# Four output buffers and eight-entry tables of destinations in the expert stage of a two-layer decoder, on one NeuronCore

## The chip, the cores and the metric

The kernel runs on one NeuronCore of a Trainium2 chip. TensorE (PE) multiplies matrices, VectorE (DVE) and ScalarE (ACT) compute and copy, GpSimd (POOL) here issues the indirect DMAs, and SyncE (SP) issues the plain ones. Each engine runs its own stream of instructions and waits for semaphores of the others. The metric is the device time of one execution in microseconds (us), as the median of the runs.

## The reference

Two decoder layers on 2048 tokens and 16 meta tokens with 1024 features. Each layer is an attention (windowed in the first, latent in the second) followed by a mixture of experts. The change is in the experts:

```python
g_p, g_idx = lax.top_k(g_prob, 1)                    # 1 of 4 groups
e_p, e_idx = lax.top_k(e_prob, TOP_K)                # 2 of its 8 experts
weights = g_p * e_p / jnp.sum(e_p, axis=-1, keepdims=True)
...
def expert_block(args):                              # w_gate, w_up: 1024x256, w_down: 256x1024
    xb, e = args
    return (jax.nn.silu(xb @ w_gate[e]) * (xb @ w_up[e])) @ w_down[e]
y = jax.ops.segment_sum(y_buf[dest] * sw[:, None], st, num_segments=T)
```

Each token goes to 2 of 32 experts; their outputs, times the token's share, are added to its row of the residual `h`.

## The kernel before

A layer's program is `project_and_route`, `experts`, `experts_beyond` (for experts with more than 160 tokens). `experts` takes the experts one after the other, 32 in layer 0 and 33 in layer 1 (`N`; the last one is a further block of an overfull expert), 160 token slots each (`CAP`; the first 128 and the other 32 are handled apart, as `x` and `xr`, `y` and `yr`). Every engine has its own `step(e)`, written as a pipeline: in step e

- PE flips the tokens of expert e (L1444, L1449), does gate and up of expert e-1 (L1461, `G` and `U`), and the down product of expert e-2 (L1475 to L1477 for 128 tokens, L1482 for the other 32). The down weights are used in two parts, `wd_hi` and `wd_lo`, which together hold them in full precision.
- ACT copies the flipped tokens (L1300, L1302), makes `wd_hi` of expert e-2 (L1309), the silu of e-1 (L1314), and half of the scaled output of e-2 (`y` L1320, `yr` L1322).
- DVE reads the list of e+2 (`find_sources`, L1339), copies flipped tokens (L1403), makes `wd_lo` of e-2 (L1329), writes the destinations and shares of e+1 (`find_places`, L1347 to L1349, semaphore `listed`), makes `h` of e-1 (L1417 to L1422), and the other half of `y` of e-2 (L1427).
- POOL gathers the tokens of e+2 (L1265, L1267) and scatters expert e-2 (L1285, L1288): an indirect DMA that adds rows of `y` and `yr` to `h` in HBM at the places of `prow`. Before it issues one scatter it waits until the scatter ahead has landed (L1283), since two that add to the same row must not overlap.
- SP loads the slots of e+2 (L1222, L1224), the gate and up weights of e (L1248, L1249) and the down weights of e-1 (L1254), 1 MB each, into rings of four buffers. It waits for `listed` of expert e-2 ahead of the slots, and for the gate and up product of e-4 ahead of the weights.

`At` holds the arithmetic of buffers: expert e has buffer e mod 2 (`slot`) or e mod 4 (`slot4`), and `uses`, `uses4` count how often that buffer was used before. `over_steps` writes the first steps out, runs the middle ones as a loop of `unroll` steps per turn, and writes out the last ones.

`prow` and `share` have four entries. The scatter of expert e-3 reads `prow` while it is issued, so DVE waits ahead of the destinations of e+1 until the scatter of e-3 has landed (L1346). `y` and `yr` have two buffers, so ACT and DVE wait ahead of expert g's output for the scatter of g-2 (L1317, L1425). `wd_hi` and `wd_lo` have one buffer: ACT waits ahead of the cast for the down product of g-1 (L1308).

Of the kernel before, what the change touches and what calls it, by code (L numbers as in the profile page):

```python
# [7 lines left out]
F32 = mybir.dt.float32  # L8
F32R = mybir.dt.float32r
# [41 lines left out]
class At:  # L51
# [1084 lines left out]
def experts(nc, io, dram, keep, layer):  # L1136


    with ExitStack() as ctx:
# [67 lines left out]
        with nc.Block() as block:  # L1207
# [49 lines left out]
            @block.gpsimd  # L1257
            def _(pool):
                def gather(e):

                    pool.wait_ge(sources, e.count(1, 1))
                    if e.after(4):
                        pool.wait_ge(flipped, e.back(4).count(3, 3))
                    pool.sem_inc(held, 1)
                    pool.indirect_dma_start(x[:, e.slot4, :], None, dram["xn"],  # L1265
                                            bass.IndirectOffsetOnAxis(ap=grow[:, e.slot4, 0:1], axis=0)).then_inc(x_in[e.slot4], 16)
                    pool.indirect_dma_start(xr[:, e.slot4, :], None, xn_parts,  # L1267
                                            bass.IndirectOffsetOnAxis(ap=grow[:, e.slot4, 1:2], axis=0)).then_inc(xr_in[e.slot4], 16)

                def step(e):  # L1270
                    if e.c == 0:
                        gather(e)
                        gather(e.back(-1))
                    if e.back(-2).live(N):
                        gather(e.back(-2))
                    f = e.back(2)
                    if f.live(N):
                        pool.wait_ge(y_act, f.count(2, 2))
                        pool.wait_ge(y_dve, f.count(1, 1))
                        pool.wait_ge(listed, f.count(1, 1))  # L1280
# [4 lines left out]
                        pool.indirect_dma_start(dram["h"], bass.IndirectOffsetOnAxis(ap=prow[:, f.slot4, 0:1], axis=0),  # L1285
                                                y[:, f.slot, :], None, bounds_check=ROWS - 1, oob_is_err=False,
                                                compute_op=ALU.add).then_inc(y_out[f.slot], 16)
                        pool.indirect_dma_start(h_parts, bass.IndirectOffsetOnAxis(ap=prow[:, f.slot4, 1:2], axis=0),  # L1288
                                                yr[:, f.slot, :], None, bounds_check=QN * ROWS - 1, oob_is_err=False,
                                                compute_op=ALU.add).then_inc(y_out[f.slot], 16)  # L1290
                over_steps(pool, 0, 2 + N, 6, EXPERTS - 2, step, unroll=4)
                for b in range(2):
                    pool.wait_ge(y_out[b], 32 * ((N + 1 - b) // 2))

            @block.scalar
            def _(act):
                def step(e):
                    if e.live(N):
                        act.wait_ge(flipped, e.count(3, 1))
                        nc.scalar.copy(xT[:, e.slot, 0:4, 0:P], T[:, e.c % 2, :].rearrange("p (c t) -> p c t", t=P)).then_inc(x_act, 1)  # L1300
                        act.wait_ge(flipped, e.count(3, 3))
                        nc.scalar.copy(xT[:, e.slot, :, P:CAP].rearrange("p (j k) t -> p k j t", k=DC // QN),  # L1302
                                       T[:, e.c % 2, 0:P * DC // QN].rearrange("p (k j t) -> p k j t", j=QN, t=REST)).then_inc(x_act, 1)
                    f, g = e.back(1), e.back(2)
                    if g.live(N):
                        act.wait_ge(d_in[g.slot4], (g.uses4 + 1) * 16)
                        if g.after(1):
                            act.wait_ge(downed, g.back(1).count(3, 3))  # L1308
                        nc.scalar.copy(wd_hi[:, :, :].rearrange("p c f -> p (c f)"), wd[:, g.slot4, :, :].rearrange("p c f -> p (c f)")).then_inc(d_high, 1)  # L1309
                    if f.live(N):  # L1310
                        act.wait_ge(gated, f.count(1, 1))
                        if f.after(2):
                            act.wait_ge(h_ready, f.back(2).count(1, 1))
                        nc.scalar.activation(act_g[:, f.slot, :, :].rearrange("p c t -> p (c t)"), G[:, f.slot, 0:FC * CAP], ACT.Silu).then_inc(silued, 1)  # L1314
                    if g.live(N):
                        if g.after(2):
                            act.wait_ge(y_out[g.slot], g.uses * 32)  # L1317
                        act.wait_ge(downed, g.count(3, 1))
                        act.wait_ge(listed, g.count(1, 1))
                        nc.scalar.activation(y[:, g.slot, 0:512], Y[:, g.c % 2, :], ACT.Copy, scale=share[:, g.slot4, 0:1]).then_inc(y_act, 1)  # L1320
                        act.wait_ge(downed, g.count(3, 3))
                        nc.scalar.activation(yr[:, g.slot, :], Y[:, g.c % 2, 0:QD4], ACT.Copy, scale=share[:, g.slot4, 1:2]).then_inc(y_act, 1)  # L1322
                over_steps(act, 0, 2 + N, 4, EXPERTS, step, unroll=4)

            @block.vector
            def _(dve):
# [15 lines left out]

                def find_places(e):

                    if e.after(4):
                        dve.wait_ge(y_out[e.slot], (e.uses - 1) * 32)  # L1346
                    nc.vector.tensor_scalar(prow[:, e.slot4, 1:2], slot[:, e.slot4, 1, 0:1], float(QN), quarter[:, :], ALU.mult, ALU.add)  # L1347
                    nc.vector.tensor_copy(prow[:, e.slot4, 0:1], slot[:, e.slot4, 0, 0:1])
                    nc.vector.tensor_copy(share[:, e.slot4, :], slot[:, e.slot4, :, 1].bitcast(F32))  # L1349
                    dve.drain().then_inc(listed, 1)  # L1350

                def along(t, of, width):
# [41 lines left out]
                def step(e):  # L1394
# [9 lines left out]
                    f, g = e.back(1), e.back(2)  # L1404
                    if g.live(N):
                        dve.wait_ge(d_high, g.count(1, 1))
                        low_part(wd_lo[:, :, :].rearrange("p c f -> p (c f)"), wd[:, g.slot4, :, :].rearrange("p c f -> p (c f)"),
                                 wd_hi[:, :, :].rearrange("p c f -> p (c f)")).then_inc(d_split, 1)
                    if e.back(-1).live(N):
                        find_places(e.back(-1))  # L1410
                    if e.turn is None and 1 <= e.c <= 10:
# [9 lines left out]
                        dve.drain()  # L1421
                        low_part(h_lo[:, f.slot, :, :], h[:, f.slot, :, 0:P], h_hi[:, f.slot, :, :]).then_inc(h_ready, 1)  # L1422
                    if g.live(N):
                        if g.after(2):
                            dve.wait_ge(y_out[g.slot], g.uses * 32)  # L1425
                        dve.wait_ge(downed, g.count(3, 2))
                        nc.vector.tensor_scalar(y[:, g.slot, 512:D], Y[:, (1 + g.c) % 2, :], share[:, g.slot4, 0:1], None, ALU.mult).then_inc(y_dve, 1)  # L1427
                over_steps(dve, 0, 2 + N, 12, EXPERTS - 4, step, unroll=4)

            @block.tensor  # L1430
            def _(pe):
                pe.wait_ge(consts, 32)

                def step(e):
# [30 lines left out]
                    if g.live(N):  # L1465
                        pe.wait_ge(d_split, g.count(1, 1))
                        pe.wait_ge(h_ready, g.count(1, 1))
                        for b in range(2):
                            if g.after(1):
                                pe.wait_ge(y_act if b else y_dve, g.count(2 if b else 1, 0))  # L1470
                            for k in range(FC):
                                hi, lo = h_hi[:, g.slot, k, :], h_lo[:, g.slot, k, :]
                                w = slice(512 * b, 512 * b + 512)
                                to = Y[:, (b + g.c) % 2, :]
                                nc.tensor.matmul(to, hi, wd_hi[:, k, w], start=(k == 0), stop=False)  # L1475
                                nc.tensor.matmul(to, hi, wd_lo[:, k, w], start=False, stop=False)
                                last = nc.tensor.matmul(to, lo, wd_hi[:, k, w], start=False, stop=(k == FC - 1))  # L1477
# [1103 lines left out]
```

## Time and profile before

| | |
|---|---|
| median of 3 runs | 3476.66 us (3474.6 to 3479.86) |
| the profiled execution's own time | 3475.05 us |
| its span, first to last instruction | 3473.2 us |
| granted TensorE clock, mean | 0.955 of full speed |
| PE, DVE, ACT, POOL busy | 3150.6, 1678.1, 1257.9, 1802.9 us |
| expert stage of layer 0, from the first slot load to the first instruction of the next stage | 885.9 to 1395.0 us |
| expert stage of layer 1, silus of the steps in the pipeline | 2940.2 to 3397.6 us |

A busy PE is a PE with matmuls in its pipeline, not one at its peak. Names begin with the stage: `ex_` is the expert stage, `aa_`, `pr_`, `pb_`, `ab_` and `fi_` are the others. Start times are counted from the span's start.

### The profile page before, as it was taken

To read this page: it belongs to the slowest core of one execution; us is meant where nothing else is said; L and a number is where in the kernel's file an instruction comes from. 1 tells how busy PE (TensorE), PEld (TensorE's weight loads), DVE (VectorE), ACT (ScalarE), POOL (GpSimd) and SP (SyncE) were. 2 spreads that over 40 slices of the span, in tenths; PEclk is the share of its full clock that TensorE was granted. 3 is DMA by queue.
4 is the path that set the end of the run, shared out by engine and by line. 5 is a ranking of instruction groups with operands and counts; after the bars stand their busy time and mean duration, and the time that the engine had idled before them with its cause. 6 is when DMAs were issued, how large, how long until landed. Compare 5 with 4: busy or idle time off the path is not lost. (4 is left out here: it accounts for less than half of the span.)

```text
span 3473.2 us, 56972 instructions
## 1 busy us (share of the span) xinstructions
PE 3150.6 (91%) x19621; PEld 2483.2 (71%) x19621; DVE 1678.1 (48%) x4096; ACT 1257.9 (36%) x2675; POOL 1802.9 (52%) x1447
## 2 busy tenths in 40 slices
PE   6999998899699998699799999999997996999992
PEld 4788886687588887699565666666665885888881
DVE  3555555577343333455365555555543663333333
ACT  2444444322122332344344444444433221322322
POOL 2655554244343333244488898888873223343344
PEclk8999999999899999799799999999999997999996
DMA  2001100843789995555602210222004545999985
GB/s 103 27 27 40 40 34 32 242 156 128 254 267 279 306 285 160 148 158 155 164 10 53 53 37 26 53 53 53 10 10 154 190 139 199 285 272 294 302 252 212
DMA packets 359637, 491.66 MB, mean 142 GB/s; under 512 B 87309, under 2 KB 286753, under 8 KB 357144
## 3 DMA queue, kind: packets, MB, share of 16 engines
q1 hardware_dynamic: 326136, 412.83, 38.0%
q0 software_dynamic: 33312, 76.43, 8.4%
q8 instruction: 104, 1.70, 0.2%
q14 instruction: 85, 0.70, 0.1%
HBM read 362.79 MB, written 135.09 MB: 143 GB/s over the span
## 5 line engine op out<-in xcount | busy, mean ns | idle before, releaser
L2117 POOL TENSOR_TENSOR ab_acc<-ab_acc,ab_pT 128x1024 f32<-128x1024 f32 (+2 forms) x320 | 593.9, 1856 | 91.7 <-ACT ab_pT L2151 53.6
L2151 ACT ACTIVATE ab_pT<-ab_S 128x512 f32<-128x512 f32 (+4 forms) x704 | 350.1, 504 | 515.2 <-PE ab_S L2242 249.8
L1285 POOL DMA_INDIRECT scratch_h<-ex_y,ex_prow x65 | 136.9, 2106 | 523.4 <-DVE ex_y L1427 370.9
L2174 DVE TENSOR_REDUCE ab_mx<-ab_W 128x2 f32<-128x800 f32 (+1 forms) x224 | 249.8, 1117 | 217.2 <-PE ab_W L2256 212.5
L1461 PE MATMUL ex_U<-ex_xT,ex_wu 128*128 128x160 f32 x2080 | 293.2, 299 | 0.0
L1461 PEld LDWEIGHTS ex_U<-ex_xT,ex_wu 128*128 128x128 f32 x2080 | 286.1, 190 | 0.0
L2240 PE MATMUL ab_S<-ab_q_hi,ab_k_hi 97*128 97x512 f32 (+4 forms) x704 | 276.0, 392 | 4.4 <-ACT ab_pT L2151 2.8
L2289 PE MATMUL ab_O<-ab_pT,ab_v 128*64 128x512 f32 (+3 forms) x1280 | 261.5, 547 | 0.0
L2241 PE MATMUL ab_S<-ab_q_lo,ab_k_hi 96*128 96x512 f32 (+4 forms) x704 | 255.1, 362 | 0.0
L2242 PE MATMUL ab_S<-ab_q_hi,ab_k_lo 96*128 96x512 f32 (+4 forms) x704 | 253.4, 360 | 0.0
L1085 PE MATMUL pr_PR<-pr_wo_hi,pr_o_hi 128*128 128x512 f32 x528 | 217.1, 411 | 38.0 <-DVE pr_wo_lo L950 33.5
L1347 DVE TENSOR_SCALAR ex_prow<-ex_slot,ex_quarter 128x1 int32<-128x1 int32 x65 | 13.8, 213 | 487.1 <-DMA scratch_h<-ex_yr,ex_prow 486.9
L333 POOL TENSOR_TENSOR aa_prob<-aa_prob,aa_rden 128x1024 f32<-128x1024 f32 x68 | 127.3, 1894 | 191.6 <-DVE aa_rden L500 191.6
L2256 PE MATMUL ab_W<-ab_k_hi,ab_q_hi 96*128 96x512 f32 (+5 forms) x704 | 206.5, 378 | 17.1 <-ACT ab_k_hi L2139 14.2
L1086 PE MATMUL pr_PR<-pr_wo_lo,pr_o_hi 128*128 128x512 f32 x528 | 211.1, 400 | 0.0
L1087 PE MATMUL pr_PR<-pr_wo_hi,pr_o_lo 128*128 128x512 f32 x528 | 211.0, 400 | 0.0
L2240 PEld LDWEIGHTS ab_S<-ab_q_hi,ab_k_hi 97*128 97x128 f32 x704 | 135.6, 193 | 87.3 <-issue 56.3
L2289 PEld LDWEIGHTS ab_O<-ab_pT,ab_v 128*64 128x64 f32 x1280 | 86.7, 139 | 139.9 <-issue 110.5
L1314 ACT ACTIVATE ex_act_g<-ex_G 128x320 f32<-128x320 f32 x65 | 28.4, 438 | 431.1 <-PE ex_U L1461 431.1
L589 PE MATMUL aa_PRJ<-aa_w_hi,aa_x_hi 128*128 128x512 f32 (+1 forms) x408 | 155.5, 381 | 16.3 <-DVE aa_w_lo L514 7.2
L2170 DVE CUSTOM_DVE_ANT_0 ab_junk<-ab_W,ab_mask 128x128 bf16<-128x128 f32 (+6 forms) x256 | 109.6, 466 | 125.1 <-PE ab_W L2256 123.8
L1329 DVE TENSOR_TENSOR ex_wd_lo<-ex_wd,ex_wd_hi 128x2048 fp32r<-128x2048 f32 x65 | 149.3, 2297 | 22.5 <-ACT ex_wd_hi L1309 22.3
(298 smaller groups left out, 7511.0 us busy)
## 6 DMA issues: line engine op xcount, KB each, us to landing
ex_wu<-in_moe_w_up SPq DMA_DIRECT2D x65, 1024.0 KB, 14.0
ex_wd<-in_moe_w_down SPq DMA_DIRECT2D x65, 1024.0 KB, 15.5
keep_wg<-in_moe_w_gate SPq DMA_DIRECT2D x33, 1024.0 KB, 8.0
ring_wg<-in_moe_w_gate SPq DMA_DIRECT2D x32, 1024.0 KB, 7.2
pr_o<-scratch_oT SPq DMA_DIRECT2D x33, 512.0 KB, 4.8
scratch_h<-pr_h SPq DMA_DIRECT2D x33, 512.0 KB, 5.1
scratch_xn<-pr_xn SPq DMA_DIRECT2D x33, 512.0 KB, 2.7
scratch_qT<-pb_qT SPq DMA_DIRECT2D x17, 768.0 KB, 5.2
```

What stands on the lines that cost most here:

```text
L1085: nc.tensor.matmul(PR[:, b, :], o_hi[:, i.slot, c, :], wo_hi[:, c, w], start=(c == 0), stop=False)
L1086: nc.tensor.matmul(PR[:, b, :], o_hi[:, i.slot, c, :], wo_lo[:, c, w], start=False, stop=False)
L1087: return nc.tensor.matmul(PR[:, b, :], o_lo[:, i.slot, c, :], wo_hi[:, c, w], start=False, stop=(c == DC - 1))
L1461: last = nc.tensor.matmul(out[:, f.slot, CAP * k:CAP * k + CAP], w[:, f.slot4, c, P * k:P * k + P], xT[:, f.slot, c, :], start=(c == 0), s ...
L2117: nc.gpsimd.tensor_tensor(to, to, pT[:, U % RING, :, 0:n], ALU.add).then_inc(added, 1)
L2151: nc.scalar.activation(pT[:, U % RING, h, 0:n], S[:, h, 0:n], ACT.Exp, scale=B_SCALE).then_inc(exped, 1)
L2174: nc.vector.reduce_max(mx[:, :, t, c:c + 1].rearrange("p h a -> p (h a)"), W[:, j % 2, :, 0:n], AX.X).then_inc(emptied, 1)
L2240: nc.tensor.matmul(to, k_hi[:, p % 2, h, kb], q_hi[:, p % 2, h, qs], start=True, stop=False)
L2241: nc.tensor.matmul(to, k_hi[0:QD, p % 2, h, kb], q_lo[:, p % 2, h, qs], start=False, stop=False)
L2242: last = nc.tensor.matmul(to, k_lo[:, p % 2, h, kb], q_hi[0:QD, p % 2, h, qs], start=False, stop=not diagonal)
L2256: last = nc.tensor.matmul(W[:, j % 2, h, 0:n], q_hi[0:QD, p % 2, h, P * t:P * t + P], k_hi[0:QD, p % 2, h, lo:lo + n], start=True, stop=True)
L2289: last = nc.tensor.matmul(O[HD * h:HD * h + HD, G % 2, 512 - n:512], values(U, h), pT[:, U % RING, h, 0:n], start=(U == opens[p, g]), stop ...
```

## The change

The tables `prow` and `share` get eight entries in place of four, `y` and `yr` four buffers in place of two (with four semaphores `y_out` for two), `wd_hi` and `wd_lo` two in place of one. Each wait that guards a buffer looks back as far as the new number of buffers says. The loops of POOL, ACT and DVE take eight steps per turn, so that the number of an entry is fixed in each written step; `uses4` is made right for that. PE's loop and SP's stay at four.

```diff
     @property
     def uses4(self):
 
-        return self.c // 4 if self.turn is None else self.turn + self.c // 4
+        return self.c // 4 if self.turn is None else self.turn * (self.unroll // 4) + self.c // 4
+
+    @property
+    def slot8(self):
+        return self.c % 8
...
-        wd_hi, wd_lo = s.sb("wd_hi", [P, FC, D], F32R), s.sb("wd_lo", [P, FC, D], F32R)
+        wd_hi, wd_lo = s.sb("wd_hi", [P, 2, FC, D], F32R), s.sb("wd_lo", [P, 2, FC, D], F32R)
...
-        prow = s.sb("prow", [P, 4, 2], I32)
-        share = s.sb("share", [P, 4, 2])
+        prow = s.sb("prow", [P, 8, 2], I32)
+        share = s.sb("share", [P, 8, 2])
...
-        y = s.sb("y", [P, 2, D])
-        yr = s.sb("yr", [P, 2, QD4])
+        y = s.sb("y", [P, 4, D])
+        yr = s.sb("yr", [P, 4, QD4])
...
-        y_out = s.sems("y_out", 2)
+        y_out = s.sems("y_out", 4)
...
                         d = f.back(1)
                         if f.after(1):
-                            pool.wait_ge(y_out[d.slot], (d.uses + 1) * 32)
+                            pool.wait_ge(y_out[d.slot4], (d.uses4 + 1) * 32)
...
-                over_steps(pool, 0, 2 + N, 6, EXPERTS - 2, step, unroll=4)
-                for b in range(2):
-                    pool.wait_ge(y_out[b], 32 * ((N + 1 - b) // 2))
+                over_steps(pool, 0, 2 + N, 6, EXPERTS - 2, step, unroll=8)
+                for b in range(4):
+                    pool.wait_ge(y_out[b], 32 * ((N + 3 - b) // 4))
...
-                        if g.after(1):
-                            act.wait_ge(downed, g.back(1).count(3, 3))
+                        if g.after(2):
+                            act.wait_ge(downed, g.back(2).count(3, 3))
...
-                        if g.after(2):
-                            act.wait_ge(y_out[g.slot], g.uses * 32)
+                        if g.after(4):
+                            act.wait_ge(y_out[g.slot4], g.uses4 * 32)
...
-                over_steps(act, 0, 2 + N, 4, EXPERTS, step, unroll=4)
+                over_steps(act, 0, 2 + N, 8, EXPERTS, step, unroll=8)
...
-                    if e.after(4):
-                        dve.wait_ge(y_out[e.slot], (e.uses - 1) * 32)
+                    if e.after(8):
+                        dve.wait_ge(y_out[e.slot4], (e.uses4 - 1) * 32)
...
-                        if g.after(2):
-                            dve.wait_ge(y_out[g.slot], g.uses * 32)
+                        if g.after(4):
+                            dve.wait_ge(y_out[g.slot4], g.uses4 * 32)
...
-                over_steps(dve, 0, 2 + N, 12, EXPERTS - 4, step, unroll=4)
+                over_steps(dve, 0, 2 + N, 12, EXPERTS - 4, step, unroll=8)
```

The rest of the diff puts the new buffer numbers into the operands.

No instruction changes its place among its engine's others; what changes is which semaphore some of them wait for, and after how many steps a loop turns. First VectorE in layer 0, from its `wd_lo` of expert 6 to its half of that expert's output, in step 8. A semaphore's number was used by an earlier stage, and the rows give it that stage's name: `aa_copied_dve` and `aa_copied_act` are `y_out[0]` and `y_out[1]`, `aa_summed` and `aa_o_ready` are the two new ones. Before:

```order
L1329 TENSOR_TENSOR ex_wd_lo<-ex_wd,ex_wd_hi 128x2048 [waits aa_sink_exped]
L1347 TENSOR_SCALAR ex_prow<-ex_slot,ex_quarter 128x1 [waits aa_copied_dve]
L1348 COPY ex_prow<-ex_slot 128x1
L1349 COPY ex_share<-ex_slot 128x2
L1381 TENSOR_REDUCE ex_ahead<-ex_grid 1x32
L1382 TENSOR_SCALAR ex_whose<-ex_whose 1x32
L1417 TENSOR_TENSOR ex_h<-ex_act_g,ex_U 128x320 [waits aa_exped,aa_scaled]
L1420 CAST ex_h_hi<-ex_h 128x256
L1329 TENSOR_TENSOR ex_h_lo<-ex_h,ex_h_hi 128x256
L1427 TENSOR_SCALAR ex_y<-ex_Y,ex_share 128x512 [waits aa_scaled,aa_copied_act]
```

The same place of the changed kernel:

```order
L1333 TENSOR_TENSOR ex_wd_lo<-ex_wd,ex_wd_hi 128x2048 [waits aa_sink_exped]
L1351 TENSOR_SCALAR ex_prow<-ex_slot,ex_quarter 128x1 [waits aa_summed]
L1352 COPY ex_prow<-ex_slot 128x1
L1353 COPY ex_share<-ex_slot 128x2
L1385 TENSOR_REDUCE ex_ahead<-ex_grid 1x32
L1386 TENSOR_SCALAR ex_whose<-ex_whose 1x32
L1421 TENSOR_TENSOR ex_h<-ex_act_g,ex_U 128x320 [waits aa_exped,aa_scaled]
L1424 CAST ex_h_hi<-ex_h 128x256
L1333 TENSOR_TENSOR ex_h_lo<-ex_h,ex_h_hi 128x256
L1431 TENSOR_SCALAR ex_y<-ex_Y,ex_share 128x512 [waits aa_scaled,aa_o_ready]
```

The order is the same line by line. Ahead of the destinations (L1347, now L1351) it waited for the scatter of expert 5 through `y_out[1]` in odd steps, of expert e-3 in general, and waits now for expert e-7's through one of four semaphores.

## Rows read from the trace of the kernel before

**Rows 1.** The page, a costly group: count, busy, mean ns, idle before and its releaser.

```profile
L1347 DVE TENSOR_SCALAR ex_prow<-ex_slot,ex_quarter 128x1 int32<-128x1 int32 x65 | 13.8, 213 | 487.1 <-DMA scratch_h<-ex_yr,ex_prow 486.9
```

**Rows 2.** Waits of 942 to 1346 us: total us, times, longest us.

```profile
DVE ex_prow L1347 <- DMA scratch_h<-ex_yr,ex_prow: 234.5, 27, 10.5
...
PE ex_Y L1475 <- DVE ex_wd_lo L1329: 12.3, 10, 1.9
...
DVE ex_wd_lo L1329 <- ACT ex_wd_hi L1309: 3.5, 2, 2.2
```

**Rows 3.** Waits of 2958 to 3378 us, TensorE's for VectorE.

```profile
PE ex_Y L1475 <- DVE ex_wd_lo L1329: 11.8, 8, 2.7
```

**Rows 4.** Timeline of one step: start us, duration us, instruction, idle before.

```profile
1157.67 1.61 POOL L1285 DMA_INDIRECT scratch_h<-ex_y,ex_prow  x1 [7.91 <-DVE ex_y L1427]
...
1164.30 1.07 PE L1482 MATMUL ex_Y<-ex_wd,ex_h 128*32 128x256 f32 x16
...
1167.38 1.90 ACT L1309 CAST ex_wd_hi<-ex_wd 128x2048 fp32r<-128x2048 f32 x1
1169.09 0.21 DVE L1347 TENSOR_SCALAR ex_prow<-ex_slot,ex_quarter 128x1 int32<-128x1 int32 x1 [9.10 <-DMA scratch_h<-ex_yr,ex_prow]
...
1170.99 0.74 DVE L1427 TENSOR_SCALAR ex_y<-ex_Y,ex_share 128x512 f32<-128x512 f32 x1
...
1172.74 2.33 DVE L1329 TENSOR_TENSOR ex_wd_lo<-ex_wd,ex_wd_hi 128x2048 fp32r<-128x2048 f32 x1
1172.75 1.61 POOL L1285 DMA_INDIRECT scratch_h<-ex_y,ex_prow  x1 [8.72 <-issue]
...
1175.50 0.50 PE L1475 MATMUL ex_Y<-ex_wd_hi,ex_h_hi 128*128 128x512 f32 x1
```

**Rows 5.** Timeline of ScalarE's L1302, once per TensorE step, early in layer 0.

```profile
942.65 0.37 ACT L1302 COPY ex_xT<-ex_T 128x256 f32<-128x256 f32 x1 [0.53 <-PE ex_T L1449]
...
957.06 0.37 ACT L1302 COPY ex_xT<-ex_T 128x256 f32<-128x256 f32 x1 [0.53 <-PE ex_T L1449]
...
971.36 0.37 ACT L1302 COPY ex_xT<-ex_T 128x256 f32<-128x256 f32 x1 [0.53 <-PE ex_T L1449]
...
985.55 0.37 ACT L1302 COPY ex_xT<-ex_T 128x256 f32<-128x256 f32 x1 [0.53 <-PE ex_T L1449]
```

**Rows 6.** The silus by line, steps of 920 to 1360 and of 2936 to 3390 us.

```profile
L1314 ACT ACTIVATE ex_act_g<-ex_G x30: 437/437/440, 922.9 to 1354.1; 128x320 f32<-128x320 f32 x30
...
L1314 ACT ACTIVATE ex_act_g<-ex_G x31: 437/438/439, 2940.2 to 3384.9; 128x320 f32<-128x320 f32 x31
```

**Rows 7.** Windows: us, busy us PE, PEld, DVE, ACT, POOL, clock, DMA share, GB/s.

```profile
926.00:1345.00 419.00, 399.72 (x2881) 347.73 (x2871) 156.58 (x317) 122.98 (x170) 165.29 (x110) 1.00 0.94 287
...
1042.00:1046.00 4.00, 4.00 (x12) 2.81 (x10) 0.00 (x0) 0.69 (x1) 3.39 (x3) 0.58 1.08 359
...
3104.80:3146.40 41.60, 40.88 (x299) 35.77 (x299) 15.95 (x34) 13.07 (x18) 16.63 (x12) 1.00 1.00 307
```

**Rows 8.** Timeline ahead of that low clock: TensorE waits for VectorE.

```profile
1041.59 0.50 PE L1475 MATMUL ex_Y<-ex_wd_hi,ex_h_hi 128*128 128x512 f32 x1 [1.85 <-DVE ex_wd_lo L1329]
```

**Rows 9.** Timeline: two scatters three steps apart; the longest landing of a scatter.

```profile
3104.83 1.61 POOL L1285 DMA_INDIRECT scratch_h<-ex_y,ex_prow  x1 [7.65 <-DVE ex_y L1427]
...
3146.41 1.61 POOL L1285 DMA_INDIRECT scratch_h<-ex_y,ex_prow  x1 [7.30 <-DVE ex_y L1427]
...
3321.91 3.68 POOL L1285 DMA_INDIRECT scratch_h<-ex_y,ex_prow  x1 [7.98 <-DVE ex_y L1427]
...
3335.51 0.21 DVE L1347 TENSOR_SCALAR ex_prow<-ex_slot,ex_quarter 128x1 int32<-128x1 int32 x1 [11.41 <-DMA scratch_h<-ex_yr,ex_prow]
```

**Rows 10.** Timeline of the last steps of layer 0's experts.

```profile
1370.94 1.89 ACT L1309 CAST ex_wd_hi<-ex_wd 128x2048 fp32r<-128x2048 f32 x1
...
1375.21 0.80 PE L1475 MATMUL ex_Y<-ex_wd_hi,ex_h_hi 128*128 128x512 f32 x1 [4.70 <-DVE ex_wd_lo L1329]
```

**Rows 11.** SyncE's own waits, 900 to 1360 us.

```profile
SPq L1222 <- DVEq L1350: 224.0, 24, 11.6
```

More of the change, by code:

```diff
@@ L1306, in step @@
                         act.wait_ge(d_in[g.slot4], (g.uses4 + 1) * 16)
-                        if g.after(1):
-                            act.wait_ge(downed, g.back(1).count(3, 3))
-                        nc.scalar.copy(wd_hi[:, :, :].rearrange("p c f -> p (c f)"), wd[:, g.slot4, :, :].rearrange("p c f -> p (c f)")).then_inc(d_high, 1)
+                        if g.after(2):
+                            act.wait_ge(downed, g.back(2).count(3, 3))
+                        nc.scalar.copy(wd_hi[:, g.slot, :, :].rearrange("p c f -> p (c f)"), wd[:, g.slot4, :, :].rearrange("p c f -> p (c f)")).then_inc(d_high, 1)
                     if f.live(N):
@@ L1315, in step @@
                     if g.live(N):
-                        if g.after(2):
-                            act.wait_ge(y_out[g.slot], g.uses * 32)
+                        if g.after(4):
+                            act.wait_ge(y_out[g.slot4], g.uses4 * 32)
                         act.wait_ge(downed, g.count(3, 1))
                         act.wait_ge(listed, g.count(1, 1))
-                        nc.scalar.activation(y[:, g.slot, 0:512], Y[:, g.c % 2, :], ACT.Copy, scale=share[:, g.slot4, 0:1]).then_inc(y_act, 1)
+                        nc.scalar.activation(y[:, g.slot4, 0:512], Y[:, g.c % 2, :], ACT.Copy, scale=share[:, g.slot8, 0:1]).then_inc(y_act, 1)
                         act.wait_ge(downed, g.count(3, 3))
-                        nc.scalar.activation(yr[:, g.slot, :], Y[:, g.c % 2, 0:QD4], ACT.Copy, scale=share[:, g.slot4, 1:2]).then_inc(y_act, 1)
-                over_steps(act, 0, 2 + N, 4, EXPERTS, step, unroll=4)
+                        nc.scalar.activation(yr[:, g.slot4, :], Y[:, g.c % 2, 0:QD4], ACT.Copy, scale=share[:, g.slot8, 1:2]).then_inc(y_act, 1)
+                over_steps(act, 0, 2 + N, 8, EXPERTS, step, unroll=8)
             @block.vector
@@ L1343, in find_places @@
                 def find_places(e):
-                    if e.after(4):
-                        dve.wait_ge(y_out[e.slot], (e.uses - 1) * 32)
-                    nc.vector.tensor_scalar(prow[:, e.slot4, 1:2], slot[:, e.slot4, 1, 0:1], float(QN), quarter[:, :], ALU.mult, ALU.add)
-                    nc.vector.tensor_copy(prow[:, e.slot4, 0:1], slot[:, e.slot4, 0, 0:1])
-                    nc.vector.tensor_copy(share[:, e.slot4, :], slot[:, e.slot4, :, 1].bitcast(F32))
+                    if e.after(8):
+                        dve.wait_ge(y_out[e.slot4], (e.uses4 - 1) * 32)
+                    nc.vector.tensor_scalar(prow[:, e.slot8, 1:2], slot[:, e.slot4, 1, 0:1], float(QN), quarter[:, :], ALU.mult, ALU.add)
+                    nc.vector.tensor_copy(prow[:, e.slot8, 0:1], slot[:, e.slot4, 0, 0:1])
+                    nc.vector.tensor_copy(share[:, e.slot8, :], slot[:, e.slot4, :, 1].bitcast(F32))
                     dve.drain().then_inc(listed, 1)
@@ L1406, in step @@
                         dve.wait_ge(d_high, g.count(1, 1))
-                        low_part(wd_lo[:, :, :].rearrange("p c f -> p (c f)"), wd[:, g.slot4, :, :].rearrange("p c f -> p (c f)"),
-                                 wd_hi[:, :, :].rearrange("p c f -> p (c f)")).then_inc(d_split, 1)
+                        low_part(wd_lo[:, g.slot, :, :].rearrange("p c f -> p (c f)"), wd[:, g.slot4, :, :].rearrange("p c f -> p (c f)"),
+                                 wd_hi[:, g.slot, :, :].rearrange("p c f -> p (c f)")).then_inc(d_split, 1)
                     if e.back(-1).live(N):
@@ L1474, in step @@
                                 to = Y[:, (b + g.c) % 2, :]
-                                nc.tensor.matmul(to, hi, wd_hi[:, k, w], start=(k == 0), stop=False)
-                                nc.tensor.matmul(to, hi, wd_lo[:, k, w], start=False, stop=False)
-                                last = nc.tensor.matmul(to, lo, wd_hi[:, k, w], start=False, stop=(k == FC - 1))
+                                nc.tensor.matmul(to, hi, wd_hi[:, g.slot, k, w], start=(k == 0), stop=False)
+                                nc.tensor.matmul(to, hi, wd_lo[:, g.slot, k, w], start=False, stop=False)
+                                last = nc.tensor.matmul(to, lo, wd_hi[:, g.slot, k, w], start=False, stop=(k == FC - 1))
                             last.then_inc(downed, 1)
```

14 lines of the change are left out of this document (7 added, 7 removed).

## The prediction

> **What bounds the kernel now.** I read the page first, then the waits inside each expert stage, then one step in order of time. On the page VectorE's largest idle time in the experts stands ahead of the destinations (`find_places`): 486.9 us over both layers until a scatter landed [rows 1], 8.7 us in each of the 27 steps that the waits of layer 0 cover [rows 2]. VectorE has slack, so this alone costs nothing. What matters is who waits for VectorE: TensorE does, ahead of the down product, for `wd_lo`, 10 times in layer 0 (12.3 us) and 8 times in layer 1 (11.8 us) [rows 2, 3].
>
> The timeline shows the ring that makes VectorE late [rows 4]. POOL issues a scatter at 1157.67. It lands, and VectorE's destinations start at 1169.09, 11.4 us later. Behind them stand `h`, which TensorE needs a step later, and the other half of `y` at 1170.99, and on that waits the next scatter, issued at 1172.75. So scatter, destinations, `y`, scatter goes round in 15.1 us: 11.4 us for the landing and 3.7 us for VectorE and the hand-overs. `wd_lo` of the next step stands behind that `y` on VectorE.
>
> TensorE alone is quicker. ScalarE's L1302 follows TensorE's flips once per step; early in layer 0, where nobody waits, it starts at 942.65, 957.06, 971.36 and 985.55 [rows 5]: 14.41, 14.30 and 14.19 us. The first two lie about the turn of TensorE's loop, every fourth step, so a step costs 14.19 us and a turn 0.33 us (0.22 and 0.11). Whenever the ring is longer than that, VectorE falls back until TensorE has to wait. What TensorE loses is then the stage's time over its floor. The silus, one per TensorE step, give it [rows 6]: 29 steps in 431.2 us in layer 0, where 29 times 14.19 are 411.5 and 7 turns 2.3, so 17.4 us too many; 30 steps in 444.7 us in layer 1, less 425.7 and 2.3, so 16.7 us. Together 34.1 us. Of these 24.1 are the waits of [rows 2, 3]. The rest is the refilling of the pipeline behind each wait and the clock: after TensorE had sat idle for 1.85 us ahead of 1041.59 [rows 8], the granted clock was 0.58 over 1042 to 1046 [rows 7], nearer the 1.2 GHz level than the 2.4 GHz one at which it is granted 1.00 elsewhere.
>
> **The change part by part.** *Eight entries of `prow` and `share`.* VectorE waits for the scatter of e-7 in place of e-3. That one was issued four steps earlier still, and even the longest landing I found, 13.6 us [rows 9], is over in one. The wait goes, 8.7 us a step. What VectorE waits for next is the silu of e-1, at the end of TensorE's gate and up product, so it runs beside TensorE with 5.6 us of work per 15 us step (156.58 us in 419 [rows 7]: 28.1 steps of 14.9). `wd_lo` is then ready after ScalarE's cast (1167.38 and 1.90 us [rows 4]) and its own 2.33 us, by 1171.6; the down product that needs it starts at 1175.50 [rows 4]. Margin 3.9 us. Gain: all of the 34.1 us, if nothing else becomes the bound.
>
> *Four buffers of `y` and `yr`.* ACT and VectorE wait for the scatter of g-4 in place of g-2. The scatter of g-2 has landed by then already, since POOL never has two scatters under way and VectorE has waited for the next one, g-1, a few rows ahead; gain 0 by itself. With two buffers the wait of L1425 would become the guard once L1346's is gone, but one scatter further back, so it too would seldom bind.
>
> *Two buffers of `wd_hi` and `wd_lo`.* ACT's cast waits for the down product of g-2 in place of g-1. But ahead of the cast ACT's stream has L1302, which waits for flips that TensorE does after that down product (the cast starts at 1167.38, L1482 ended at 1165.4 [rows 4]); the wait never ends last. In the last steps, without flips, the cast, at 1370.94 [rows 10], stands behind `yr` of g-1 in ACT's stream, which waits for the same down product. So 0, and the 4.70 us that TensorE waits there [rows 10] stay, once per layer.
>
> *The scatter chain.* POOL still issues a scatter only when the one ahead has landed. That chain now has no VectorE in it: landing 11.4 us and some 0.1 us to go on; POOL's two gathers lie inside the landing. It is shorter than 14.19 us, so it is hidden behind TensorE; uncovered it would cost what it is over 14.27 us (14.19 and a quarter of 0.33), times 59 steps.
>
> *SyncE.* Its slots wait for `listed`, 224.0 us in 24 waits [rows 11], 9.3 us each. With `listed` early it waits for the gate and up product of e-4 instead, and the weights start some 9 us sooner, with the same ring. TensorE never waited for weights, so this gains 0; it presses on the DMA engines, below.
>
> *Loops of eight steps.* The same instructions, fewer turns; ACT writes four more steps out. VectorE, ACT and POOL have slack: between 0 and, by TensorE's own turn, 0.33 us for each of at most 4 turns per layer, off the path. I take 0.
>
> Sum against the profiled execution's own time: 3475.05 - 34.1 = 3441.0 us. The median of the runs is 1.6 us above that execution, so 3442.6, and I say 3443.
>
> **DMA, the disputed cost.** The rows give two bounds. With 14.9 us steps the DMA share is 0.94 (926 to 1345), 287 GB/s, so 14.0 us of DMA time and 4.28 MB per step. In three steps of 13.86 us (scatters at 3104.83 and 3146.41 [rows 9]) the share was 1.00 at 307 GB/s [rows 7], again 4.26 MB, and the scatters kept landing in time. So 13.9 us per step has been seen and 14.27 asks for 299 GB/s at a share of 0.98. The share can read up to 1.08 (1042 to 1046, at 359 GB/s [rows 7]), so the engines have between 0.4 and 1.3 us of room per step (14.27 less 13.9, and 14.27 less 14.0 over 1.08). I take it that they keep up, but the room is small: if contention adds 4% to the DMA time, they bind. The Trainium skill, "DMA: Bandwidth & Descriptors", section "Bandwidth" ("Where 436 GB/s comes from"), puts HBM traffic of one core at about 358 GB/s; by that an estimate for 4.28 MB is 12.0 us per step, under TensorE's 14.19, and the sum would be the same. The trace agrees as far as it goes, with 359 GB/s at most.
>
> The longest landing has another cause that could grow: that scatter's issue on POOL took 3.68 us in place of 1.61 [rows 9], so up to 2.1 us may come on top of 11.4, 13.5 in all, still under 14.27. The skill's page "SBUF — State Buffer", section "Who interferes with whom", says that GpSimd and a VectorE copy in its two-port form lock each other out of a shared port for a whole instruction, which fits such an issue. By that rule VectorE's copies, moved some 8 us, hit other DMA issues than now; that shifts waits of 2 us in a chain with 2.8 us of room, and the sum stays.
>
> **The rivals.**
> *A. The DMA engines take over, partly* (17%). Against it 13.86 us steps seen; for it shares of 0.98 to 1.00 over a whole layer, never seen that long. If a step settles halfway between now (14.9) and the floor, at 14.6, 0.3 us times 59 is left of the gain: 34 - 18 = 16 us, so 3461; over the range of such settlings 3451 to 3468.
> *B. The wait is only renamed* (8%). VectorE was late for another reason, or DMA needs 14.9 us per step once weights and scatters overlap more. Against it: VectorE waited for ScalarE's cast only twice, 3.5 us [rows 2]. Time 3470 to 3484.
> *C. Slower* (4%). The weights no longer start after a landing but with TensorE's product, and run beside each scatter; if that lengthens the landing beyond 14.9 us, POOL's own chain is slower than the ring of today. It would take 3.5 us more than the 11.4 of now and 1.3 more than the longest; at 15.3 us, 0.4 us times 59 is +24: 3500. Below 14.27 it costs nothing.
> *D. The change does as computed* (71%): 3438 to 3450, with up to 2 us of spread between runs below and a few unhidden hand-overs above.
>
> **How the numbers follow.** The time is D's, 3443. The range reaches from 3438, as there is no way below TensorE's floor but the spread of runs, over D and most of A to 3461; B, C and the top of A, 20%, are left out. A measurement of this kernel can tell about 0.2%, 7 us: D and A are faster by more (0.88), B mostly within (0.08), C slower (0.04).
>
> **What the profile would show.** Right: no wait of VectorE for a scatter at the destinations, instead about 5 us a step for the silu; TensorE's waits for `wd_lo` gone but for the one at each layer's end; 29 silu steps in 414 us and 30 in 428; scatters issued every 14.2 to 14.4 us; DMA share about 0.98. SyncE waits for gate and up, not for `listed`. Wrong: TensorE waits for a weight or gather DMA (A), POOL's scatters are released by the scatter ahead and not by `y` (C), or VectorE still comes late to `wd_lo`, behind something else (B).

## The result, and the profile after

The changed kernel takes 3433.31 us (median of 4 runs, 3430.81 to 3438.2) beside 3475.63 us before (4 runs, 3463.84 to 3479.86). The ratio is 0.9885, with a 95% interval of 0.9859 to 0.9912. That is 42 us less (31 to 49 by the interval), and below the range of the prediction, which ended at 3438. When both were timed again it was 3439.04 beside 3473.2 us, 34 us less (experiment 1). The profiled execution took 3430.81 us, the quickest of its four.

The silus of the changed kernel, one per TensorE step, with count, shortest, median and longest in ns, and first and last start; first layer 0, then layer 1. They answer to [rows 6]:

```profile
L1318 ACT ACTIVATE ex_act_g<-ex_G x30: 437/438/441, 921.0 to 1334.7; 128x320 f32<-128x320 f32 x30
...
L1318 ACT ACTIVATE ex_act_g<-ex_G x31: 437/438/441, 2913.8 to 3341.7; 128x320 f32<-128x320 f32 x31
```

29 steps now take 413.7 us where they took 431.2, and 30 steps 427.9 where they took 444.7: 17.5 and 16.8 us less. The sum of floor and loop turns was 413.8 and 428.0. The steps are at the floor that the prediction worked out.

The waits of the changed kernel, 922 to 1326 us of layer 0 (total us, times, longest). They answer to [rows 2]:

```profile
DVE ex_h L1421 <- ACT ex_act_g L1318: 117.6, 28, 4.8
...
DVE ex_wd_lo L1333 <- ACT ex_wd_hi L1313: 61.2, 28, 2.2
```

The list of this stretch has no line of VectorE waiting for a scatter, and none of TensorE waiting for `wd_lo`. VectorE waits for the silu instead, 4.2 us a step, and ahead of `wd_lo` for ScalarE's cast, which was late only twice before. It is paced by TensorE now, not by the landing. `wd_lo` is ready well ahead: at 1145.03 us in one step of the changed kernel, whose down product starts at 1148.90. What is left for TensorE is the end of the layer (waits of 900 to 1400 us), as in [rows 10]:

```profile
PE ex_Y L1479 <- DVE ex_wd_lo L1333: 4.7, 1, 4.7
```

The windows of the changed kernel over its steps, columns as in [rows 7], and SyncE's waits (900 to 1340 us), which answer to [rows 11]:

```profile
922.00:1326.00 404.00, 397.07 (x2892) 348.00 (x2891) 162.04 (x323) 123.76 (x172) 163.62 (x111) 1.00 0.96 299
2915.00:3342.00 427.00, 419.82 (x3058) 369.06 (x3057) 169.63 (x335) 130.53 (x180) 172.42 (x116) 1.00 0.95 294
```

```profile
SPq L1226 <- DVEq L1354: 124.0, 22, 6.1
SPq L1252 <- PE ex_U L1465: 78.1, 24, 10.2
SPq L1258 <- PE ex_Y L1486: 70.3, 24, 13.9
```

The DMA engines carry 299 GB/s at a share of 0.96, and SyncE waits for three things where it waited for hardly more than one.

Where are the 44.3 us that the two profiled spans differ by (3473.2 and 3428.9)? The first slot load and the last scatter of the experts bound each expert stage. Before, both layers' starts and the last scatter of layer 1 are at these rows of its timeline:

```profile
885.94 0.34 SPq L1222 DMA_DIRECT2D ex_slot<-scratch_slot  x1
...
2903.32 0.34 SPq L1222 DMA_DIRECT2D ex_slot<-scratch_slot  x1
...
3413.94 1.55 POOL L1285 DMA_INDIRECT scratch_h<-ex_y,ex_prow  x1 [6.55 <-ACT ex_yr L1322]
```

After:

```profile
883.66 0.34 SPq L1226 DMA_DIRECT2D ex_slot<-scratch_slot  x1
...
2876.20 0.34 SPq L1226 DMA_DIRECT2D ex_slot<-scratch_slot  x1
...
3369.87 1.55 POOL L1289 DMA_INDIRECT scratch_h<-ex_y,ex_prow  x1 [5.63 <-ACT ex_yr L1326]
```

The expert stage of layer 1 went from 510.6 to 493.7 us, and by the same rows of layer 0 (its last scatters at 1383.1 and 1362.8) that stage went from 497.2 to 479.1. That is 35.0 us of the 44.3. The other 9.3 lie outside these two stretches, nearly all in stages whose code the diff doesn't touch, 2.3 of them before the first expert. The table gives the same split for every profiled execution of this study:

| profiled execution | expert stages, layer 0 + 1 | all the rest of the span |
|---|---|---|
| before | 497.2 + 510.6 = 1007.8 | 2465.4 |
| changed | 479.1 + 493.7 = 972.8 | 2456.1 |
| changed, again (experiment 1) | 479.8 + 493.8 = 973.6 | 2462.3 |
| loops of eight only (2) | 497.6 + 516.0 = 1013.6 | 2460.6 |
| tables of eight only (3) | 480.1 + 494.1 = 974.2 | 2469.1 |
| output and weight buffers only (4) | 493.9 + 513.6 = 1007.5 | 2462.4 |
| `find_places` last only (5) | 480.0 + 494.2 = 974.2 | 2465.3 |
| cast ahead (6) | 476.4 + 490.1 = 966.5 | 2462.9 |
| more to load (7) | 480.7 + 493.7 = 974.4 | 2464.7 |
| flips between, cast ahead (8) | 459.7 + 473.7 = 933.4 | 2467.8 |
| flips between, small buffers (9) | 460.0 + 472.6 = 932.6 | 2462.0 |
| flips between, cast not ahead (10) | 477.5 + 491.9 = 969.4 | 2464.0 |

Where the steps are at the floor, the expert stages repeat within 2 us (972.8 to 974.4 in the five such profiles with the old order of the flips and the cast). With the ring still closed they lie 6 us apart (1007.5 to 1013.6). The rest moves between 2456.1 and 2469.1 with no visible relation to what was changed, and the first profile of the changed kernel happens to hold its lowest value.

### The profile page after: what moved, and what is told of

Its sections match the earlier page's. It is cut to its first block and busy times, and to the rows that moved or that the text cites. A ratio compares the mean times of both kernels' runs of the same rounds, so it can differ in the third digit from the quotient of the medians.

```text
span 3428.9 us, 56794 instructions
## 1 busy us (share of the span) xinstructions
PE 3136.8 (91%) x19621; PEld 2478.4 (72%) x19621; DVE 1683.2 (49%) x4096; ACT 1258.0 (37%) x2675; POOL 1795.6 (52%) x1447
## 5 line engine op out<-in xcount | busy, mean ns | idle before, releaser
L1289 POOL DMA_INDIRECT scratch_h<-ex_y,ex_prow x65 | 104.4, 1607 | 495.8 <-ACT ex_yr L1326 293.3
L1421 DVE TENSOR_TENSOR ex_h<-ex_act_g,ex_U 128x320 f32<-128x320 f32 x65 | 31.7, 488 | 282.1 <-ACT ex_act_g L1318 282.1
```

## The experiments

Each was timed in five rounds against the kernel before on the same chip.

### 1. The changed kernel again

> The changed kernel once more, to tell how much of its 42 us lies inside the expert stages and how much is spread. Theory R (ring only, the rest is spread between executions): 3433 to 3443 us, 33 to 42 below the kernel before on the same chip; the 29 and 30 silu steps take 413.7 and 427.9 us again, within 0.3, while the other stages move by several us against the first profile. Theory L (the written-out code of eight steps also moves the other stages): 3431 to 3436, and latent attention again 4 us shorter than in the profile of before.

Measured: 3439.04 us (3436.79 to 3441.41) beside 3473.2 for before, whose 23 runs reach from 3465.19 to 3484.06. Ratio 0.99, interval 0.9881 to 0.9919. The 29 and 30 silu steps take 413.9 and 428.1 us, within 0.2 of the first profile. The expert stages take 973.6 us beside 972.8, the rest 2462.3, 6 us more than in the first profile. That is theory R. Latent attention took 926.7 us before, 922.4 in the first profile of the changed kernel and 923.5 here, so it alone doesn't tell R from L.

### 2. Only the loops of eight

```diff
-        return self.c // 4 if self.turn is None else self.turn + self.c // 4
+        return self.c // 4 if self.turn is None else self.turn * (self.unroll // 4) + self.c // 4
...
-                over_steps(pool, 0, 2 + N, 6, EXPERTS - 2, step, unroll=4)
+                over_steps(pool, 0, 2 + N, 6, EXPERTS - 2, step, unroll=8)
...
-                over_steps(act, 0, 2 + N, 4, EXPERTS, step, unroll=4)
+                over_steps(act, 0, 2 + N, 8, EXPERTS, step, unroll=8)
...
-                over_steps(dve, 0, 2 + N, 12, EXPERTS - 4, step, unroll=4)
+                over_steps(dve, 0, 2 + N, 12, EXPERTS - 4, step, unroll=8)
```

> Loops of eight steps on POOL, ACT and DVE with all the old buffers and waits. Theory R: nothing, 3475 us within 7, silu steps of 431 and 445 us as before. Theory L: 4 to 9 us less than before, all of it outside the expert stages.

Measured: 3480.17 us (12 runs, 3471.13 to 3493.16), ratio 1.0018, interval 1.0004 to 1.0031. The written-out code gives nothing; if anything it costs 6 us. In the profile 6 us more stand in the expert stages (1013.6 beside 1007.8 us), where the ring sets the pace; experiment 4 has the same loops and 1007.5 there, so the loops alone don't explain them. Theory L is out: what the changed kernel gained outside the experts did not come from the code's length.

### 3. Only the tables of eight

```diff
-        prow = s.sb("prow", [P, 4, 2], I32)
-        share = s.sb("share", [P, 4, 2])
+        prow = s.sb("prow", [P, 8, 2], I32)
+        share = s.sb("share", [P, 8, 2])
...
-                    if e.after(4):
-                        dve.wait_ge(y_out[e.slot], (e.uses - 1) * 32)
+                    if e.after(8):
+                        dve.wait_ge(y_out[e.slot], (e.uses - 3) * 32)
```

(with the loops of eight and `slot8` in the operands)

> Eight entries of destinations and shares (and the loops of eight that they need), but two buffers of y and yr and one of the down weights' parts. The theory of the prediction: all of the gain is here, 3433 to 3443 us, silu steps in 414 and 428 us. Rival (buffers together): the wait moves to L1317 and L1425 for the scatter of g-2 and at least half of the gain is lost, 3455 us or more.

Measured: 3441.21 us (3437.92 to 3445.15), ratio 0.9902, interval 0.9882 to 0.9921, on the same chip as experiment 1. The expert stages take 974.2 us, 33.6 of the 35.0. VectorE waits for no landing in layer 0's steps, though two output buffers are all it has. The tables carry the gain, as predicted.

### 4. Only the output buffers and the parts of the down weights

```diff
-        prow = s.sb("prow", [P, 8, 2], I32)
-        share = s.sb("share", [P, 8, 2])
+        prow = s.sb("prow", [P, 4, 2], I32)
+        share = s.sb("share", [P, 4, 2])
...
-                    if e.after(8):
-                        dve.wait_ge(y_out[e.slot4], (e.uses4 - 1) * 32)
+                    if e.after(4):
+                        dve.wait_ge(y_out[e.slot4], e.uses4 * 32)
```

(a diff against the changed kernel, so with its loops of eight; `slot4` again in the operands)

> Four buffers of y and yr and two of wd_hi and wd_lo, with tables of four entries as before, so VectorE still waits for the scatter of e-3. The theory of the prediction: no gain, 3475 us within 7. Rival (the output buffers guard the ring): a third or more of the gain, 3462 us or less.

Measured: 3472.44 us, ratio 1.0006, interval 0.9992 to 1.002. Nothing. VectorE waits as before (there 220.9 us in 25 waits), as its line in the waits of 942 to 1320 us shows:

```profile
DVE ex_prow L1351 <- DMA scratch_h<-ex_yr,ex_prow: 216.2, 25, 11.6
```

### 5. The kernel before, with `find_places` last

```diff
-                    if e.back(-1).live(N):
-                        find_places(e.back(-1))
                     if e.turn is None and 1 <= e.c <= 10:
                         list_beyond(e.c)
...
                         nc.vector.tensor_scalar(y[:, g.slot, 512:D], Y[:, (1 + g.c) % 2, :], share[:, g.slot4, 0:1], None, ALU.mult).then_inc(y_dve, 1)
+                    if e.back(-1).live(N):
+                        find_places(e.back(-1))
```

> The kernel before, buffers and loops and all, with only find_places moved behind VectorE's half of y, at the end of the step. The wait for the scatter of e-3 then has nothing behind it that the next scatter needs. Theory of the prediction (it is the place of the wait in VectorE's stream, not the buffers, that closes the ring): at least 25 of the 34 us, 3440 to 3449 on a chip where before takes 3473; the wait at the destinations shrinks from 8.7 us a step to under 2. Rival (a table of four entries is too shallow wherever its wait stands, because the landing takes longer than what is left of the step): VectorE waits as long as before, just later, and the time is 3465 us or more.

Measured: 3439.46 us (3437.5 to 3442.57), ratio 0.9901, interval 0.9885 to 0.9917. With not one buffer more, two moved lines give what the whole change gives. The landing that VectorE had waited 8.7 us a step for has by now gone by while it made `h` and `y`; the waits of 926 to 1340 us have this line for it:

```profile
DVE ex_prow L1347 <- DMA scratch_h<-ex_yr,ex_prow: 0.4, 2, 0.2
```

So the ring was closed by the place of the wait. A deeper table opens it, and so does a wait behind the work that the next scatter needs.

### 6. The changed kernel, with the down weights' parts made one step ahead

```diff
-                    if g.live(N):
-                        act.wait_ge(d_in[g.slot4], (g.uses4 + 1) * 16)
-                        if g.after(2):
-                            act.wait_ge(downed, g.back(2).count(3, 3))
+                    if f.live(N):
+                        act.wait_ge(d_in[f.slot4], (f.uses4 + 1) * 16)
+                        if f.after(2):
+                            act.wait_ge(downed, f.back(2).count(3, 3))
```

(the cast and `wd_lo` take expert f = e-1 in place of g = e-2)

> The changed kernel, with the cast of the down weights and its remainder made one step ahead, into the second buffer. Theory (the second buffer is worth nothing as used, and TensorE's 4.7 us wait for wd_lo at the end of each layer is only the order on ScalarE): 9 us less than the changed kernel, 3424 to 3432 us, ex0 and ex1 4.7 us shorter each, steps in the middle at 14.19 still. Rival (the wait at the end hides another one, for silu and h of the last expert): under 4 us less. A ramp that waits for the first down weights could give 2 us back.

Measured: 3429.51 us (3427.65 to 3431.18), ratio 0.987, interval 0.9852 to 0.9889; 9.5 us less than experiment 1's median, from another chip, and 9.5 less than experiment 7's on the same one. By the stages, 7.1 us less (966.5 beside 973.6), 3.4 and 3.7, and not 4.7 each. The last scatter is up against another wait; of 1340 to 1380 us:

```profile
POOL scratch_h L1289 <- DMA scratch_h<-ex_yr,ex_prow: 3.6, 1, 3.6
```

TensorE's wait for `wd_lo` at the end is gone. POOL has the last output early and must wait for the scatter ahead to land. That is the chain of scatters, seen here for the first time as what ends last in a stage.

### 7. The changed kernel with 12% more to load

```diff
+        more = s.sb("more", [P, 2, 4, FE])
...
+                        if e.after(2):
+                            sp.wait_ge(more_in[e.slot], e.uses * 16)
+                        sp.dma_start(more[:, e.slot, :, :], weights_of("moe_w_up", e)[:, 0:4, :]).then_inc(more_in[e.slot], 16)
```

> The changed kernel with half a megabyte more to load in every step (half of the up weights a second time, into a buffer that nobody reads), 12% more bytes, to find how much room the DMA engines have. At the share of 0.96 that the changed kernel shows, a step's DMA time of 13.7 us grows to 15.3. Theory 1 (a share of 1.00 is all there is): steps of 15.3 us, 60 us more than the changed kernel, about 3500. Theory 2 (the share can go to 1.08): 14.2 us, hidden, within 5 us of the changed kernel, about 3440.

Measured: 3438.99 us (3437.19 to 3441.01), ratio 0.9898, interval 0.9879 to 0.9916: no cost that the time shows. The windows of its steps, and the one line of the waits of 926 to 1320 us in which TensorE waits for a load:

```profile
926.00:1320.00 394.00, 386.00 (x2812) 338.62 (x2812) 157.16 (x312) 120.32 (x166) 168.00 (x110) 1.00 1.05 329
...
2920.00:3330.00 410.00, 403.15 (x2933) 353.88 (x2932) 165.38 (x331) 124.52 (x172) 170.57 (x113) 1.00 1.06 332
```

```profile
PE ex_G L1470 <- DMA ex_wu<-in_moe_w_up: 0.7, 1, 0.7
```

The share stood at 1.05 for 400 us and nearly all of it was hidden. Not quite all: the 29 silu steps of layer 0 took 415.5 us where the changed kernel has 413.7, and nearly all of the 1.8 us more fell in three steps near 1300 us; the 30 of layer 1 took 427.9 as before. ScalarE's cast now waited for the down weights 9 times, 19.9 us in all over 926 to 1320 us, in slack that was free before. Theory 2 holds; a share near 1.00 did not mean that the engines were full.

### 8. Cast ahead, and the flips of `xr` between gate and up

```diff
-                        pe.wait_ge(x_act, e.count(2, 1))
-                        pe.wait_ge(xr_in[e.slot4], (e.uses4 + 1) * 16)
-                        for k in range(DC // QN):
-                            last = nc.tensor.transpose(T[:, e.c % 2, P * k:P * k + P], xr[:, e.slot4, P * k:P * k + P], ident[:, :])
-                        last.then_inc(flipped, 1)
...
+                            if out is G and e.live(N):
+                                flip_rest()
```

(a diff against experiment 6; `flip_rest` is the block taken out above)

> cast_ahead, and TensorE's two flips of xr put between the gate and the up product, so that it no longer waits for ScalarE's copy just ahead of the gate. Theory (the floor of 14.19 us holds 0.4 to 0.5 us of that wait): 13.7 to 13.8 us a step, 25 us less than cast_ahead. Rival 1 (TensorE is kept by its own work there, the wait is covered by the matmuls in flight): under 5 us less. Rival 2 (DMA engines, at 0.96 of their share, become the bound): between 5 and 20 us less, with TensorE waiting for a load or VectorE for a landing.

Measured: 3396.16 us (3392.43 to 3403.1), ratio 0.9773, interval 0.9757 to 0.9789; 33 us less than experiment 6. The silus of 920 to 1330 us, and the wait that the edit takes away, as the kernel before has it in its waits of 942 to 1346 us:

```profile
L1317 ACT ACTIVATE ex_act_g<-ex_G x30: 437/438/439, 923.4 to 1321.3; 128x320 f32<-128x320 f32 x30
```

```profile
PE ex_T L1449 <- ACT ex_xT L1300: 6.7, 28, 0.2
```

29 steps in 397.9 us, 13.72 each with the turns, where the changed kernel has 14.27. The profile's own wait ahead of these flips is 0.24 us on TensorE and 0.48 on its weight loads (13.3 us in 28 waits); 0.55 came back, and the waits of this run have no such line. Neither rival holds: the wait was not covered, and the DMA engines did not bind.

### 9. The same with the small buffers

The kernel before with the edits of experiments 5, 6 and 8: tables of four, two output buffers, loops of four, and two buffers of `wd_hi` and `wd_lo`.

> The kernel before with find_places last, two buffers of wd_hi and wd_lo filled one step ahead, and the flips of xr between gate and up; tables of four, two output buffers and loops of four as before. Theory (the tables and the output buffers aren't needed once the wait stands last): as e8_flip_between, 3392 to 3402 us, steps of 13.6 us. Rival (at 13.6 us a step the landing no longer fits behind a table of four): VectorE waits for landings again and the time is over 3405.

Measured: 3396.41 us (3392.86 to 3400.15), ratio 0.9771, interval 0.9757 to 0.9785. As experiment 8, with 29 steps in 398.3 us. The tables of eight and the four output buffers are not needed at 13.7 us a step either.

### 10. The flips between, without the cast ahead

The changed kernel with only the edit of experiment 8.

> The changed kernel with the flips of xr between gate and up, but the cast of the down weights not ahead. ScalarE's cast then starts only behind the copy of xr, at the end of the gate product, and wd_lo ends about when the down product wants it. Theory: TensorE waits for wd_lo by about 0.4 us a step and the end waits stay, so 3412 to 3430 us. Rival (there is margin still): 3405 to 3410, e8 plus the 9 us of the two ends.

Measured: 3435.67 us (3428.91 to 3437.25), ratio 0.9879, interval 0.9861 to 0.9896, above both expectations. The silus, and one step's flips of `xr` and start of the down product:

```profile
L1318 ACT ACTIVATE ex_act_g<-ex_G x30: 438/438/439, 920.2 to 1333.3; 128x320 f32<-128x320 f32 x30
```

```profile
1157.59 0.38 PE L1455 MATMUL ex_T<-ex_ident,ex_xr 128*128 128x128 f32 x2
...
1162.56 0.50 PE L1486 MATMUL ex_Y<-ex_wd_hi,ex_h_hi 128*128 128x512 f32 x1 [0.24 <-DVE ex_wd_lo L1333]
```

29 steps in 413.1 us, 14.24 each: all but 0.02 us a step of the 0.55 is gone. The flips now release ScalarE's copy, the cast and `wd_lo` only after the gate product, and `wd_lo` releases the down product and so the next flips. From the flips to the down product that chain takes 4.97 us here. In experiment 8 the same two starts are at 1151.91 and 1156.37, 4.46 us apart, with TensorE's own up product between them. So TensorE loses 0.51 us a step, of which the profile shows 0.24 us as a wait of its matmuls, in each of the 29 steps, and 0.48 as one of its weight loads. I had put the loss at 0.4 us a step; over 59 steps the missing 0.1 us is 6 to 7 us, about what the time lies above the expectation's 3430. In experiments 8 and 9 this is where the second buffer of `wd_hi` and `wd_lo` is worth something.

## Why the prediction was right and wrong

**The ring: right, in place and size.** The floor of 14.19 us, the 0.33 us turn and 34.1 us of gain: the same steps fell by 34.3 us (17.5 and 16.8). `wd_lo`'s forecast margin of 3.9 us is there too (1145.03 to 1148.90). The timed difference in experiment 1 was 34.2 us; that it agrees to 0.1 is luck, as its interval is 28 to 41 us. Experiments 3 and 4 put it on the tables; experiment 5 adds that moving the wait would have done as well. The prediction had the reason for that in its own words, that `h` and `y` stand behind the destinations, without drawing the conclusion.

**The floor: right as a number, wrong as "TensorE alone".** The prediction took 14.19 us from steps "where nobody waits". In those steps TensorE waited each time for ScalarE's copy ahead of the flips of `xr`, 28 times in 942 to 1346 us. The change leaves that wait where it is, so the sum holds. But "no way below TensorE's floor" is true of this order of instructions only: experiment 8 went 0.55 us a step below it.

**SyncE: half wrong.** It was to wait for gate and up and no longer for `listed`. It still waits for `listed`, 124.0 us in 22 waits of layer 0 where it had 224.0 in 24, and also for the down product, 70.3 us, which the prediction doesn't have. TensorE waited for no weights either way, so the sum doesn't change.

**The edits taken at nothing: right.** The four output buffers and two parts of the down weights gave 1.0006 of the time before (experiment 4), the loops of eight 1.0018 (experiment 2). The 4.70 us at each layer's end stayed. The tables alone leave 2.2 us between medians to the full change, with runs that overlap.

**The DMA engines: the mechanism right, the room too small.** The share was forecast at 0.98 and was 0.96, and rival A, at 17%, did not come. The 0.4 to 1.3 us of room per step were undersized: experiment 7 put half a megabyte more into each step, 1.7 us by an estimate from 307 GB/s at a share of 1.00 [rows 7], and hid all of it but 1.8 us in a whole layer. The long issue of a scatter, which the prediction laid to VectorE's copies, stood beside another instruction, the subtraction `wd_lo`; the last section has the rows. It didn't come again in the changed kernel's steps.

**The end of each stage: no effect of the change.** Last silu to last scatter went from 16.4 to 15.5 us in both layers, 1.8 us that the prediction doesn't have, and TensorE's granted clock in the 28 us behind the last silu was 0.77 where it had been 0.69. But the same happens without the tables: with only the loops of eight (experiment 2) the ends took 15.5 and 15.3 us at 0.78 and 0.77. And with the tables the long end comes back: experiment 3 has 16.4 us at 0.69 in layer 0 and 15.4 at 0.77 in layer 1. So the end goes with the granted clock of the execution, not with the edit; what sets that clock, no run here isolates. In the two first profiles the 1.8 us are partly made up by starts that took 1.0 us longer from the first slot load to the second silu, so that the stages fell by 35.0.

**The range: this step failed.** "The range reaches from 3438, as there is no way below TensorE's floor but the spread of runs", and that spread was put at "up to 2 us". The three runs shown already spanned 5.3 us; the fourth lay 11 us below the lowest of them, and 23 runs of the kernel before on one chip span 19 us. The profiles say where most of it is: outside the expert stages the same code took 2456.1 to 2469.1 us, and inside them the kernels with the closed ring differ by up to 6.

A gain of 35 us in the experts leaves 7 us of the first 42 for the rest, where the two profiled executions differ by 9.3. The split of the medians itself is inferred, since only one execution of each was profiled; that 34 lies inside the interval of 31 to 49 us fits it. The second comparison gave 34.2, and the medians of experiments 3, 5 and 7, whose steps are at the same floor or within 2 us of it, are 3439 to 3441 us, inside the range. So the gain was sized right. The term that was too small is the spread: the range left 5 us below the forecast of 3443, with 2 of them named as spread, and the first median came 9.7 us below it.

In which of the other stages the spread arises is open; latent attention alone varied from 922.1 to 930.1 us, at granted clocks that differ (0.99 and 1.00 in its last third for the two first profiles), but no run here controls that clock.

## What to carry to other kernels

When an engine waits for a transfer, ask what stands behind the wait in its stream and whether the next transfer needs it: that closes a ring, and moving the wait behind that work opens it without a buffer. The floor of the engine that is then the bound can be read from steps in which the other engines don't hold it longer than they do in every step, and it held to 0.1 us in 430. It is the floor of that order of instructions: a short wait that comes in every step hides in it, and moving an instruction can take it out. A range needs the spread of whole runs, which here lay mostly in stages that the change doesn't touch, and three runs were too few to show it.

## What the runs showed of the hardware

A DMA share of 0.96 to 1.00 was not a full set of engines: with 12% more to load it read 1.05 and 1.06 at 329 and 332 GB/s, and TensorE lost 1.8 us in layer 0's 29 steps and nothing in layer 1's 30.

How long POOL took to issue a scatter followed what VectorE was doing. Before, the issue took about 1.61 us or, in 16 of 65, 3.29 to 3.73 [rows 9]. In the changed kernel every one of 29 took about 1.61 (shortest, median and longest in ns):

```profile
L1289 POOL DMA_INDIRECT scratch_h<-ex_y,ex_prow x29: 1563/1612/1633, 926.2 to 1325.6; - x29
```

Before, `wd_lo` (a subtraction with two operands in SBUF) ran beside most of these issues. The order of the two starts decided. All 16 long issues began 0.04 to 0.48 us after a subtraction had; the one of 3321.91 us [rows 9] began 0.09 us after it. An issue that began ahead of the subtraction, or at most 0.04 us behind it, took its 1.61 us although the two overlapped, as at 1172.75 us, 0.01 us behind `wd_lo` [rows 4]. At 0.04 us both occur. In the changed kernel the gather meets the subtraction instead:

```profile
1142.74 2.29 DVE L1333 TENSOR_TENSOR ex_wd_lo<-ex_wd,ex_wd_hi 128x2048 fp32r<-128x2048 f32 x1 [2.19 <-ACT ex_wd_hi L1313]
1144.23 1.67 POOL L1269 DMA_INDIRECT ex_x<-scratch_xn,ex_grow  x1 [0.30 <-issue]
```

The gather begins 1.49 us behind the subtraction and ends 0.87 us after it, where a gather by itself takes 0.98 us. So an issue of POOL that begins clearly inside the subtraction seems to stand still until it ends. The Trainium skill, "SBUF — State Buffer", section "Who interferes with whom", says that a VectorE instruction with two SBUF inputs contends with GpSimd's reads, which agrees with these rows. Which part of an issue is held, no run here shows. All this was read from the timelines, not tested by itself.
